# A two-stage RWKV block on one core: the stage barrier replaced by single waits, and the readout's VectorE operations moved to GpSimd

## What is computed

```python
def wkv_scan(r, w, k, v, kk, a, s0, reverse):
    def step(S, inp):
        r_t, w_t, k_t, v_t, kk_t, a_t = inp
        sa = jnp.einsum("bhvk,bhk->bhv", S, kk_t)
        S = (S * w_t[:, :, None, :]
             - sa[..., None] * (kk_t * a_t)[:, :, None, :]
             + v_t[..., None] * k_t[:, :, None, :])
        return S, jnp.einsum("bhvk,bhk->bhv", S, r_t)
...
def rwkv7_readout(o, streams, r_k, gn_g, gn_b, w_out, out_dtype):
    mean = jnp.mean(o, axis=-1, keepdims=True)
    var = jnp.mean(jnp.square(o - mean), axis=-1, keepdims=True)
    y = ((o - mean) * lax.rsqrt(var + GN_EPS)).reshape(B, T, RW_WIDTH) * gn_g + gn_b
    bonus = jnp.sum(jnp.sum(r[:, :, None] * kd * r_k, axis=-1, keepdims=True) * v[:, :, None], axis=2)
    y = (y + bonus.reshape(B, T, RW_WIDTH)) * jax.nn.silu(g)
    return y.astype(out_dtype) @ w_out
```

## Time and profile before

| | |
|---|---|
| median of 3 runs | 2460.35 us (2456.99 to 2462.3) |
| the profiled execution | 2467.71 us, its span 2465.9 us |
| busy in the span | PE 84%, DVE 54%, ACT 45%, POOL 28% |
| mean granted TensorE clock | 0.943 |
| DMA: stores of streams, 48 | 576 KB each, 8.8 us from issue to landing (median) |
| DMA: fetches bkv and ARI, 96 each | 192 and 128 KB, 3.1 and 3.2 us |

### The profile page before, as it was taken

The page is one execution under the profiler, slowest core; times in us unless marked ns, Lnnn a source line. Parts: engine busy times, 40 slices in busy tenths (PEclk is TensorE's granted clock), DMA queues, the critical chain, the costliest instruction groups (busy, mean ns, idle before and its releaser), DMA issues.

```text
span 2465.9 us, 56685 instructions
## 1 busy us (share of the span) xinstructions
PE 2071.1 (84%) x24540; PEld 1585.2 (64%) x24540; DVE 1325.5 (54%) x2205; ACT 1119.8 (45%) x1861; POOL 681.7 (28%) x407
## 2 busy tenths in 40 slices
PE   5899999178888888787979999987898888898888
PEld 3777777167666766665767666655666665666666
DVE  2268788334344445444166666672456752466752
ACT  4367676233333333333255454552455553455552
POOL 1243443300011011023332222223434332443432
PEclk8999999589889999998999999988999998999998
DMA  7224453743432232313321111112222211222122
GB/s 289 70 88 154 134 171 91 220 115 102 114 97 67 69 77 53 80 42 146 90 90 56 52 56 52 43 35 94 68 78 72 74 60 63 74 83 71 61 69 69
DMA packets 156153, 221.33 MB, mean 90 GB/s; under 512 B 84481, under 2 KB 109313, under 8 KB 155137
## 3 DMA queue, kind: packets, MB, share of 16 engines
q1 hardware_dynamic: 144800, 174.45, 22.8%
q0 software_dynamic: 9952, 40.11, 5.4%
q10 hardware_dynamic: 1152, 3.15, 0.3%
HBM read 164.98 MB, written 42.21 MB: 84 GB/s over the span
## 4 chain that ended last, share of the span: by engine, by line
PE 40%; DVE 12%; ACT 8%; issue 6%; POOL 2%; DMA 1%; DVEq 0%; ACTq 0%; POOLq 0%; SPq 0%
PE ps L259 6%; PE ps L261 6%; PE ps L260 6%; PE ps L2279 2%; PE ps L2816 2%; PE ps L2239 1%; PE ps L2793 1%; PE ps L1372 1%; ACT p L2299 1%; PE ps L398 1%; DVE Y L1520 1%; ACT wbh L239 1%; PE ps L1362 1%; DVE pc L2882 1%; DVE Rc L352 1%
## 5 line engine op out<-in xcount | busy, mean ns | idle before, releaser
L244 POOL TENSOR_TENSOR wbl<-wb,wbh 128x1024 fp32r<-128x1024 f32 x128 | 308.6, 2412 | 649.4 <-ACT wbh L239 645.6
L259 PE MATMUL ps<-hTh,wah 128*128 128x512 f32 (+1 forms) x512 | 180.5, 353 | 17.8 <-POOL wal L244 10.7
L1520 DVE COPY_PREDICATED Y<-rc,ps 128x512 f32<-128x512 int32 x120 | 85.1, 730 | 198.0 <-ACT DE L1484 136.9
L259 PE MATMUL ps<-hT2h,wbh 128*128 128x512 f32 x416 | 180.0, 433 | 12.2 <-POOL wbl L244 12.2
L260 PE MATMUL ps<-hTl,wah 128*128 128x512 f32 (+1 forms) x512 | 174.9, 342 | 0.0
L261 PE MATMUL ps<-hTh,wal 128*128 128x512 f32 (+1 forms) x512 | 174.7, 341 | 0.0
L259 PE MATMUL ps<-hT1h,wbh 128*128 128x512 f32 (+1 forms) x432 | 168.0, 389 | 3.1 <-POOL hT1l L2420 3.1
L239 ACT ACTIVATE wbh<-wb 128x1024 fp32r<-128x1024 f32 x128 | 134.6, 1052 | 68.8 <-PE ps L1958 43.4
L261 PE MATMUL ps<-hT2h,wbl 128*128 128x512 f32 x416 | 164.5, 396 | 0.0
L260 PE MATMUL ps<-hT2l,wbh 128*128 128x512 f32 x416 | 163.7, 393 | 0.0
L346 POOL TENSOR_TENSOR ro<-ro 128x256 f32<-128x256 f32 (+1 forms) x12 | 11.9, 994 | 548.4 <-DVE ro L330 548.4
(11 more groups left out here) (402 smaller groups left out, 5351.5 us busy)
## 6 DMA issues: line engine op xcount, KB each, us to landing
wb<-in_w_in SPq DMA_DIRECT2D x56, 512.0 KB, 3.5
s_str_dram<-s POOLq DMA_DIRECT2D x48, 576.0 KB, 8.8
wm<-in_ada SPq DMA_DIRECT2D x48, 512.0 KB, 6.0
bkv<-s_str_dram SPq DMA_DIRECT2D x96, 192.0 KB, 3.1
wa<-in_rw_in SPq DMA_DIRECT2D x34, 512.0 KB, 4.2
wb<-in_da_in SPq DMA_DIRECT2D x32, 512.0 KB, 3.5
ARI<-s_str_dram SPq DMA_DIRECT2D x96, 128.0 KB, 3.2
wb<-in_w_out SPq DMA_DIRECT2D x16, 512.0 KB, 3.5
```

The lines of the kernel that those rows point to most:

```text
L244: e.tensor_tensor(self.lo[:, n % 2], self.raw[:, n % 3], self.hi[:, n % 2].bitcast(F32), ALU.subtract).then_inc(self.K.s.w_lo, 1)
L259: e.matmul(z, wh[:, k, :], hi[:, k, a:b], start=k == 0, stop=False)
L1520: e.copy_predicated(self.Y[:, l - 1], twice(self.mY[l - 1]), banks[:, :, 0:256]).then_inc(v, 1)
```

## The change

**No barrier.** `barrier` and its calls are gone. The steps prepare(0), and prepare(1) beside the first half of invert(0), become a generator `fill`, which each engine runs beside post(7), 20 steps of it to 8. What the barrier had kept apart is now kept by single waits, on buffers of Scan that lie where Mix has its own (the places in SBUF are laid out anew, with Mix's last-used buffers in front). GpSimd's clears go into `pool_prepare` of unit 0. The store of pair 6 moves from GpSimd to SP, behind unit 0's fetch and rc. The modulation's rows, turns and loads move by two units (rows with units 3 to 13, loads from u=2).

**Readout.** VectorE keeps the mean removal and the half root. GpSimd makes the correction, the two scalings and gn_g, gn_b at 128x768. The readout has one more step, and `prepared` with a readout is paced as 11 instead of 10.

```diff
-    def together(self, project, post, bonus=lambda gp: None):
+    def together(self, project, post, bonus, fill):
         run(project(0))
         for gp in range(7):
             pace((post(gp), 8), (project(gp + 1), 12))
-        run(post(7))
+        last = post(7)
+        run(some(last, 2))
+        pace((last, 8), (fill, 20))
         bonus(7)
...
-        return u // 2 - 1 if u in range(2, 13, 2) else None
+        return u // 2 - 2 if u in range(4, 15, 2) else None
...
-        return range(2 * u, 2 * u + 2) if u < 12 else ()
+        return range(2 * u - 4, 2 * u - 2) if 2 <= u < 14 else ()
...
+        if u == 1:
+            e.wait_ge(s.st_sp, 96)
         e.wait_ge(s.pp_mm, i + 2)
         e.activation(self.vax[:, w].rearrange("x k q j t -> x (k q j t)"), both, ACT.Copy).then_inc(s.pp_a, 1)
...
     def pool_prepare(self, e, u):
+        if u == 0:
+            e.wait_ge(s.prod, self.mix.W.used(33))
+            e.memset(self.NK[:, :, :, :], 0.0).then_inc(s.s_zero, 1)
+            e.memset(self.BK[:, :, 0:2], 0.0).then_inc(s.s_zero, 1)
+            yield
+            e.wait_ge(s.tables, 32)
+            e.wait_ge(s.mix_done, 26)
...
+            e.wait_ge(s.st_sp, 96)
+            e.tensor_copy(self.Y.rearrange("x l j (n t) -> x (l j n) t", t=64), eye(40)).then_inc(s.s_zero, 1)
...
+        if u == 1:
+            e.wait_ge(s.bonus_out, 16)
         for c, j in TILES:
             m = e.matmul(ps[half(j), x + c, 0:256], K.ident[half(c), half(c)], self.NK[half(c), w, j, 0:256], start=True, stop=True)
...
+        if u == 0:
+            e.wait_ge(s.st_sp, 96)
+            e.wait_ge(self.mix.bg_out[0], 64)
         for l in range(1, 5):
             e.wait_ge(*self.iv_at(u, mm=2 * l + 2))
             e.activation(self.DE[:, u % 2, 1 - l % 2, :, 0:256], banks[:, :, 0:256], ACT.Copy).then_inc(a, 1)
...
+    def fill(self, prepare, first):
+        yield from prepare(0)
+        yield from paced((some(first, 8), 8), (prepare(1), 6))
...
     def dve_readout(self, e, gp):
...
         for j, (a, b) in enumerate(self.cols):
             self.rs.dve_half(e, 2 * gp + j, K.psum[:, j, 0:b - a], sq[:, a:b], 64e-5, 64.0)
-        for j, (a, b) in enumerate(self.cols):
-            self.rs.dve_last(e, 2 * gp + j, sq[:, a:b], rr[:, a:b])
-        yield
-        e.wait_ge(self.rs.r, self.rs.done(2 * gp + 1))
-        e.tensor_tensor(o, o, rr, ALU.mult).then_inc(s.ro_v, 1)
-        e.wait_ge(s.ro_v, 2 * gp + 1)
-        e.tensor_scalar(o, o, K.Q("gn_g", gp, 1), K.Q("gn_b", gp, 1), ALU.mult, ALU.add).then_inc(s.ro_v, 1)
         yield
...
     def pool_readout(self, e, gp):
...
+        e.tensor_tensor(sq, sq, rr, ALU.mult).then_inc(s.ro_p, 1)
+        e.wait_ge(s.ro_p, p + 1)
+        e.tensor_tensor(sq, sq, rr, ALU.mult).then_inc(self.rs.p, 4)
+        e.wait_ge(self.rs.p, 2 * done)
+        e.tensor_scalar(sq, sq, -1.0, 1.5, ALU.mult, ALU.add).then_inc(self.rs.r, 2)
+        e.tensor_tensor(o, o, rr, ALU.mult).then_inc(s.ro_p, 1)
+        e.wait_ge(s.ro_p, p + 2)
+        e.wait_ge(self.rs.r, done)
+        e.tensor_tensor(o, o, sq, ALU.mult).then_inc(s.ro_p, 1)
+        e.wait_ge(s.ro_p, p + 3)
+        e.tensor_scalar(o, o, K.Q("gn_g", gp, 1), K.Q("gn_b", gp, 1), ALU.mult, ALU.add).then_inc(s.ro_p, 1)
...
     def sp(self, e):
-        K = self.K
-        e.dma_start(self.rc[:, :], K.T["rc"]).then_inc(K.s.tables, 16)
+        e.wait_ge(s.prod, self.mix.W.used(33))
         for u in range(24):
             self.sp_fetch(e, u)
+            if u == 0:
+                e.dma_start(self.rc[:, :], K.T["rc"]).then_inc(s.tables, 16)
+                self.mix.store(e, 6)
```

More of the change, by code:

```diff
@@ L132, in pace @@
             left.remove(x)
+            continue
+        yield
+def pace(*gens):
+    for _ in paced(*gens):
+        pass
 def run(gen):
@@ L1702, in sp_bg, with together @@
         if gp:
-            e.wait_ge(s.ro_p, 2 * gp)
+            e.wait_ge(s.ro_p, 6 * gp)
+        else:
+            e.wait_ge(self.mix.st_out[1], 384)
+        e.wait_ge(self.mix.bg_out[gp % 2], 16 * (gp // 2 + 1))
         e.dma_start(self.bgl[:, :, :], self.K.T["bg"][gp]).then_inc(s.bg_in0, 16)
-    def together(self, prepare, invert, chain, readout):
+    def fill(self, prepare, first):
+        yield from prepare(0)
+        yield from paced((some(first, 8), 8), (prepare(1), 6))
+    def together(self, first, prepare, invert, chain, readout):
         def prepared(u):
```

240 lines of the change are left out of this document (137 added, 103 removed).

## The result

| | before | after |
|---|---|---|
| median, first comparison | 2461.32 us (2456.99 to 2464.12, 4 runs) | 2420.85 us (2420.15 to 2423.57, 4 runs) |
| ratio, 95% interval | | 0.9823 (0.9802 to 0.9845) |
| median, a second comparison | 2467.1 us (9 runs) | 2424.56 us (5 runs), ratio 0.9823 (0.9807 to 0.9839) |
| the profiled execution | 2467.71 us, span 2465.9 us | 2420.98 us, span 2419.2 us |

The change is 1.8% faster: 40 to 43 us between medians, 46.7 us between the two profiled executions. The forecast was 2410 us, range 2393 to 2430. The time is in the range and 11 us above the forecast of 2410.

The account below looks back on a forecast made before the run. PE was taken as starved at the boundary by the barrier, busiest in the recurrence, waiting on VectorE in readouts. -37.5+7.2-20 = -50.3; 2467.7 gives 2417.4, from the median 2460.35 gives 2410 us, range 2393 to 2430.

Parts of the forecast that it names:

- The fetch of unit 0: At the boundary: first on SP's queue, so PE's first transpose comes at 432.8, or 435.5 with the whole earlier 11.2 us.
- the rival of the store: Boundary: pair 6's store ahead of unit 1's fetch on SP makes either land well after 456; gain 25, 2422 us; chance 0.13.
- The fill: Boundary between projections and recurrence: unit 1's inversion starts at 478 instead of 517.46, gaining 37.5 us, between 30 and 46.
- The waits: Hand-overs before unit 1's inversion and its fetch: 4 to some 10 us, taken as 7, including 0 to 3 for port contention.
- The lower clock: At the start of unit 1's inversion, PE comes out of a thin stretch at lower clock: 2 us taken off the gain.
- the sign of an error in the main: At the boundary: VectorE's last operation of pair 7 ending after 490 would show the prediction wrong in the main.
- The row in unit 10: Recurrence: unit 10, so far bare, gets a row of the modulation and loses 7.2 us, between 5 and 8.
- The readouts: Six recurrence units: moving VectorE's work to GpSimd gains 20 us, between 9 and 27; 3.5 per plain unit, 3.0 with a row.
- The 3.5: Gain in us for each of four plain readout units, taken from 3.3+1.1-0.8 = 3.6.
- The rival "PE bounds the readouts": Readout units: PE's 3.0 us of products are most of the excess, so only 1.5 each come back; 2421 us; chance 0.12.
- GpSimd: Readouts: eight operations, 16 us with starts, two at 2.21; nothing in a unit waits for them and VectorE isn't slowed.
- One sign of being wrong: Readouts: SP or ScalarE waiting for GpSimd's readout would show the prediction wrong in the main.

Follow-up runs that it names:

- two store runs: Changed kernel with pair 6's store on GpSimd's queue again, 2421.37 us (0.9822), or on SP behind unit 1's fetch, 2422.98 us (0.9830).
- fill only: Changed kernel with the four readout functions of the kernel before: 2436.09 us, ratio 0.9886.
- a part alone: Kernel before, barrier included, with only the changed kernel's four readout functions: 2451.29 us, ratio 0.9937.
- GpSimd twice: Changed kernel with eight more 128x768 operations on GpSimd in each of the first five readouts: 2428.27 us, ratio 0.9850.

## Why the prediction was right, and where it was not

**The fetch of unit 0**: first transpose at 432.8 predicted, 434.29 measured, from a start 1.0 later. **Unit 0's preparation**: BK's copy ends at 446.5, predicted 445.8. **The store and unit 1's fetch**: predicted near 456, measured 457.05. The bytes were the right view. What was right for the wrong reason is the rival of the store: I spoke of the order on SP's queue, and the order hardly matters (two store runs).

**The fill** was forecast at 37.5 us, between 30 and 46. Measured: 37.2 at unit 1's inversion, and 36.5 at the first update, 37.5 if the later start of the boundary is taken out. The waits were put at 7: VectorE's are 6.92 for the first Y, 0.96 and 0.57 behind it, 8.45, and two L971 beside GpSimd's copies took 3.32 instead of 1.82, which was in the margin for contention. The lower clock was not the loss there (0.90 from 485 to 497); at that place PE has a stall of 3.41 us, not foreseen. VectorE's last operation of pair 7 ended at 480.15, well before the 490 that would have been the sign of an error in the main.

**The row in unit 10** is the step that failed most plainly. I took 30.3 - 23.1 = 7.2 from the earlier trace rows. It costs 25.61 - 23.15 = 2.5: the same unit 10, with its row in after and without it before. The window that I took for the price of a row had a stall in it and the lower clock behind it, as these two lines of the kernel before show (PE's timeline, then the windows view):

```profile
617.71 0.39 PE L1394 MATMUL ps<-Y,DE 64*64 64x64 f32 x10 [1.88 <-issue]
```

```profile
617.00:627.70 10.70, 8.43 (x133) 6.45 (x133) 1.37 (x3) 3.42 (x5) 0.00 (x0) 0.68 0.63 183
```

The granted clock of the window in the earlier trace rows, 0.89 where the bare unit has 1.00, was the warning. The 4.7 us were a loss that did not come. (In fill only the same unit took 26.15, which would be 3.0.)

**The readouts** are the second mis-sized term: 20 us forecast, 14 by units, 15.5 as a part alone. A plain unit was to fall to 24 or 24.5 and fell to 25.42, "near 26, PE bounds it". The 3.5 was made of 3.3 for the late Y and 1.1 for the clock, less 0.8. The late Y and the clock are both won (PE waits 0.17 where it waited 2.94, the clock is 1.00 where it was 0.94). What was not in the sum is that the readout's two products, 1.49 us each from start to start, fill the place that comes free: 2.3 of their 3.0 us show (25.42 - 23.15). The rival "PE bounds the readouts" had the mechanism; its price of 1.5 won for each unit was too low: the plain units won 1.8 to 2.8, 2.2 in the mean. Its time, 2421, is the one that was measured, but that is chance, since it was added up with the same wrong row and the same base as the forecast.

**GpSimd**: V took 1.21 and 1.24 us in units 12 and 13 of after, with GpSimd idle at that moment, and 1.20 in GpSimd twice, with one of the added operations beside it; QG took 1.29 for two in all three. By the rule of the Trainium skill that was cited (SBUF — State Buffer, Who interferes with whom), VectorE with at most one input in SBUF, and in no two-port mode, doesn't contend with GpSimd: the traces agree. With two, it does: L971 took 3.32 for two, L947 2.91 for one, each beside GpSimd's copy of Y. GpSimd's part is 13.4 us and not 16, because the two operations with one input took 0.83 and 0.98 us where I took 2.21 from the earlier trace rows. One sign of being wrong did come: SP waits for GpSimd's readout before it loads the next bonus and gate, as it did in the kernel before (736.93 there, right behind GpSimd's last operation). The fetch behind it waited longer for other things, so in after it cost nothing on that queue.

**The sum.** By the traces the parts give 36.5 - 2.5 + 14 = 48, and the profiled executions differ by 46.7, where 50.3 was forecast: 1.0 too much for the fill, an error of 4.7 and one of 6 with opposite signs, and 1 to 2 us of stalls and clock. That the two errors nearly cancel is luck, and so is that the other units do: units 2, 4 and 17 got 11.6 us shorter and units 0, 5, 7 and 19 13.6 longer, none of which was in the prediction. So 3.6 of the 11 us that the forecast missed are in the sum. The other 7.2 of the 11 are in the base: the profiled execution of before stood 7.4 above the median from which the sum was taken, the one of after stands at its median, and the unchanged rest was equal in the two, 1322.8. A sum made against one profiled execution and taken off a median holds only to the 5 to 10 us by which the rest varies from run to run.

## What to carry to other kernels

Before a window is taken as the price of a part, look at its granted clock and for "<-issue" in it: two windows of the same program with the same work differed by 4.5 us (25.64 and 30.13). Where "<-issue" stands, look in the DMA view for a late packet of the queue "instruction". When a wait falls away, add up what the next engine has to do in that unit; here PE's own two products took back more than half of the room. Count the bytes of a boundary before its queues: three orders of the same transfers, in four runs, ended 30.9 to 34.2 us after the last product.
